# Block compression of a sparse attention: windows as the stationary operand, four positions at once in the column groups of TensorE

## What is computed

```python
def compress(k, pos_emb, w1, w2):
    B, S, G, d = k.shape                                   # 1, 256, 2, 128
    nc = (S - CMP_LEN) // CMP_STRIDE + 1                   # 15
    idx = jnp.arange(nc)[:, None] * CMP_STRIDE + jnp.arange(CMP_LEN)[None, :]
    blocks = k[:, idx] + pos_emb[:, None, :]
    blocks = jnp.transpose(blocks, (0, 3, 1, 2, 4)).reshape(B, G, nc, CMP_LEN * d)
    return jax.nn.gelu(blocks @ w1, approximate=True) @ w2
```

## Time and profile before

| | |
|---|---|
| time, 3 runs | 2612.89 us median (2609.93 to 2614.18) |
| profiled execution: span, first to last instruction | 2603.2 us |
| median of the runs less this span | 9.7 us |
| TensorE busy | 2440.9 us, 94% |
| TensorE's weight loads | 2054.4 us, 79% |
| VectorE / ScalarE / GpSimd busy | 1418.9 / 1154.4 / 81.2 us |
| mean granted clock of TensorE | 0.955 |
| DMA | 418.71 MB, 161 GB/s in the mean |

### The profile page before, as it was taken

The page is one execution under the profiler, slowest core; times in us unless marked ns, Lnnn a source line. Parts: engine busy times, 40 slices in busy tenths (PEclk is TensorE's granted clock), DMA queues, the critical chain, the costliest instruction groups (busy, mean ns, idle before and its releaser), DMA issues.

```text
span 2603.2 us, 34397 instructions
## 1 busy us (share of the span) xinstructions
PE 2440.9 (94%) x12224; PEld 2054.4 (79%) x12224; DVE 1418.9 (55%) x1718; ACT 1154.4 (44%) x1620; POOL 81.2 (3%) x77
## 2 busy tenths in 40 slices
PE   6999987889999999999979996869899999999997
PEld 5887886768888788888868885658788888888886
DVE  4444336556666545666554445885555544455544
ACT  4444224445555444554444444334444444444432
POOL 1000100000000000000000001320000000000000
PEclk9999758989999999999989998889899999999999
DMA  7665330545555565665656652004466566665663
GB/s 228 193 191 163 98 129 5 166 130 186 186 185 175 190 192 171 193 193 193 191 159 189 193 161 65 1 25 153 128 186 185 186 192 190 190 185 182 208 193 105
DMA packets 298549, 418.71 MB, mean 161 GB/s; under 512 B 15263, under 2 KB 181465, under 8 KB 297701
## 3 DMA queue, kind: packets, MB, share of 16 engines
q1 hardware_dynamic: 295744, 407.09, 50.5%
q0 software_dynamic: 2144, 8.40, 1.0%
q10 hardware_dynamic: 580, 2.20, 0.2%
HBM read 415.52 MB, written 2.12 MB: 160 GB/s over the span
## 4 chain that ended last, share of the span: by engine, by line
PE 84%; issue 8%; DVE 5%; ACT 2%; POOL 1%; DMA 0%; ACTq 0%; DVEq 0%; POOLq 0%
PE PS L1289 22%; PE PS L1257 14%; PE PS L1256 14%; PE PS L1255 14%; PE PS L1290 11%; PE PS L1367 2%; PE PS L1302 1%; PE PS L1528 1%; DVE x L930 1%; DVE attT L1195 1%; DVE proj L1188 0%; PE PS L1304 0%; DVE proj L1192 0%; PE PS L1407 0%; PE PS L1344 0%
## 5 line engine op out<-in xcount | busy, mean ns | idle before, releaser
L806 DVE TENSOR_TENSOR wlo<-stage,whi 128x1024 fp32r<-128x1024 f32 (+2 forms) x452 | 540.3, 1199 | 625.1 <-ACT whi L529 625.0
L1289 PE MATMUL PS<-actT,whi 128*128 128x512 f32 x2432 | 859.7, 397 | 0.0
L529 ACT ACTIVATE whi<-stage 128x1024 fp32r<-128x1024 f32 (+2 forms) x452 | 467.2, 1037 | 679.6 <-PE PS L1257 656.4
L1290 PE MATMUL PS<-actT,wlo 128*128 128x256 f32 x2432 | 683.4, 281 | 0.0
L1289 PEld LDWEIGHTS PS<-actT,whi 128*128 128x128 f32 x2432 | 457.2, 188 | 112.9
L835 DVE TENSOR_TENSOR wlo<-stage,whi 128x1024 fp32r<-128x1024 f32 x298 | 358.5, 1223 | 232.5 <-ACT whi L580 230.3
L1290 PEld LDWEIGHTS PS<-actT,wlo 128*128 128x128 f32 x2432 | 456.5, 188 | 0.1
L580 ACT ACTIVATE whi<-stage 128x1024 fp32r<-128x1024 f32 x298 | 309.0, 1055 | 271.1 <-PE PS L1290 256.7
L1257 PE MATMUL PS<-whi,actT 128*128 128x512 f32 (+2 forms) x992 | 384.5, 388 | 0.0
L1255 PE MATMUL PS<-whi,actT 128*128 128x512 f32 (+2 forms) x992 | 383.8, 387 | 0.0
L1256 PE MATMUL PS<-wlo,actT 128*128 128x512 f32 (+2 forms) x992 | 381.7, 385 | 0.0
(11 more groups left out here) (249 smaller groups left out, 1605.3 us busy)
## 6 DMA issues: line engine op xcount, KB each, us to landing
stage<-in_w_up SPq DMA_DIRECT2D x304, 512.0 KB, 4.3
stage<-in_w_down SPq DMA_DIRECT2D x216, 512.0 KB, 4.7
stage<-in_w_in SPq DMA_DIRECT2D x168, 512.0 KB, 3.5
stage<-in_w_out SPq DMA_DIRECT2D x64, 512.0 KB, 4.8
stage<-in_cmp_k_w SPq DMA_DIRECT2D x8, 512.0 KB, 4.1
stage<-in_cmp_v_w SPq DMA_DIRECT2D x8, 512.0 KB, 5.1
x<-in_x ACTq DMA_DIRECT2D x2, 1024.0 KB, 6.9
grow<-bias_by_distance POOLq DMA_DIRECT2D x2, 1024.0 KB, 7.7
```

The lines of the kernel that those rows point to most:

```text
L529: nc.scalar.activation(whi[:, s % SPLITS, 0:wd], stage[:, s % STAGES, 0:wd], ACT.Copy)\
L806: nc.vector.tensor_tensor(wlo[:, s % SPLITS, 0:wd], stage[:, s % STAGES, 0:wd], whi[:, s % SPLITS, 0:wd].bitcast(F32), ALU.subtract).then_ ...
L1289: nc.tensor.matmul(o, whi[:, j % SPLITS, at], actT[:, k, :], start=k == 0, stop=False)
L1290: last = nc.tensor.matmul(o[:, S:2 * S], wlo[:, j % SPLITS, at], actT[:, k, 0:S], start=False, stop=k == KC - 1)
```

## The change

The operands of the first product change places. The 32 window columns of one position (2 groups x 16, the sixteenth a column of zeros) are now the stationary operand, and the 256 weight columns of that position move. A product with 32 stationary columns fills a quarter of the array's columns; the four positions of a tile are written to four column groups, that is to PSUM partitions 0-31, 32-63, 64-95 and 96-127 of one bank (bank 6 for keys, 7 for values). Each group sums its own eight positions, so four partial sums remain, with windows on partitions and hidden units along the row.

ScalarE copies these partial sums to SBUF (`part`), for the keys in step 4 and the values in step 8. In step 8 four small products with four stacked 32 x 32 identities (`stack`) add the four partial sums and turn the result at once (`hidden`); one gelu then covers keys and values. The window row in SBUF is now 32 wide, with a memset for the zero column, and `stack` is a further DMA at the start.

```diff
+    c["stack"] = np.tile(np.eye(32, dtype=np.float32), (4, 1))
...
+        part = sb("part", [P, 2, HID], F32, mixer1)
+        stack = sb("stack", [P, 32], F32, mixer1)
...
+            pool.dma_start(stack[:, :], w["stack"]).then_inc(ev("stack_in"), 16)
             for j, nm in enumerate(("lambda_q1", "lambda_q2", "lambda_k1", "lambda_k2")):
...
             pool.wait_ge(ev("cols"), 1)
+            pool.memset(blocks[:, :, :, :, NC:NC + 1].rearrange("p v l g c -> p (v l g) c"), 0.0).then_inc(ev("blocks_done"), 1)
...
-                        pool.tensor_tensor(blocks[:, v, 16 * a:16 * a + 16, g, :], src, add, ALU.add).then_inc(ev("blocks_done"), 1)
+                        pool.tensor_tensor(blocks[:, v, 16 * a:16 * a + 16, g, 0:NC], src, add, ALU.add).then_inc(ev("blocks_done"), 1)
...
                     act.wait_ge(ev("tile_used"), used(G["cmp"].first + STAGES * (v + 1)))
-                    nc.scalar.activation(hid[:, v, :, :], PS[:, 6:8, 0:2 * NC], ACT.Gelu_apprx_tanh).then_inc(ev("hid_done"), 1)
+                    nc.scalar.activation(part[:, v, :], PS[:, 6 + v, 0:HID], ACT.Copy).then_inc(ev("part_out"), 1)
                 if s == 8:
+                    act.wait_ge(ev("hidden_mm"), 1)
+                    nc.scalar.activation(hid, PS[:, 6, 0:P].rearrange("p (v a c) -> p v a c", v=2, a=2),
+                                         ACT.Gelu_apprx_tanh).then_inc(ev("hid_done"), 1)
...
+            def hidden():
+                pe.wait_ge(ev("part_out"), 2)
+                for n in range(4):
+                    last = nc.tensor.matmul(PS[:, 6, n * 32:(n + 1) * 32], part[:, n // 2, n % 2 * P:(n % 2 + 1) * P], stack[:, :],
+                                            start=True, stop=True)
+                last.then_inc(ev("hidden_mm"), 1)
...
-                    pe.wait_ge(ev("blocks_done"), 4 * (v + 1))
-                    if v:
-                        pe.wait_ge(ev("hid_done"), 1)
+                    pe.wait_ge(ev("blocks_done"), 4 * (v + 1) + 1)
...
                             k = FC * (j % STAGES) + l
-                            for a in range(2):
-                                at = stage[:, j % STAGES, l * HID + a * P:l * HID + (a + 1) * P]
-                                last = nc.tensor.matmul(PS[:, 6 + a, 0:2 * NC], at,
-                                                        blocks[:, v, k, :, :].rearrange("p g c -> p (g c)"),
-                                                        start=k == 0, stop=k == CMP_LEN - 1)
+                            last = nc.tensor.matmul(PS[32 * l:32 * l + 32, 6 + v, 0:HID],
+                                                    blocks[:, v, k, :, :].rearrange("p g c -> p (g c)"),
+                                                    stage[:, j % STAGES, l * HID:(l + 1) * HID],
+                                                    start=j % STAGES == 0, stop=j % STAGES == STAGES - 1)
...
                 if s == 8:
+                    pe.wait_ge(ev("stack_in"), 16)
+                    hidden()
                     pe.wait_ge(ev("w2_in"), 32)
-                    pe.wait_ge(ev("hid_done"), 2)
+                    pe.wait_ge(ev("hid_done"), 1)
```

More of the change, by code:

```diff
@@ L189, in build @@
         urow = work[0:16, 2048:2048 + SK]
-        blocks = grow[:, 0:2 * CMP_LEN * NKV * NC].rearrange("p (v l g c) -> p v l g c", v=2, l=CMP_LEN, g=NKV)
+        blocks = grow[:, :].rearrange("p (v l g c) -> p v l g c", v=2, l=CMP_LEN, g=NKV)
         w2 = proj[:, 0, C_KC:C_KC + 512].rearrange("p (v a n) -> p v a n", v=2, a=2)
-        hid = proj[:, 1, C_KC:C_KC + 4 * 2 * NC].rearrange("p (v a c) -> p v a c", v=2, a=2)
-        kcT = proj[:, 1, C_KC + 128:C_KC + 128 + 2 * NC]
+        hid = proj[:, 1, C_KC:C_KC + 4 * 32].rearrange("p (v a c) -> p v a c", v=2, a=2)
+        kcT = proj[:, 1, C_KC + 128:C_KC + 128 + 32]
         vc = proj[0:NC, 1, C_KC + 192:C_KC + 192 + NKV * P].rearrange("p (g d) -> p g d", g=NKV)
@@ L1008, in compressed @@
                     dve.wait_ge(ev("kc_mm"), 1)
-                    nc.vector.tensor_copy(kcT, PS[:, 7, 0:2 * NC])
+                    nc.vector.tensor_copy(kcT, PS[:, 7, 0:32])
                     nc.vector.tensor_copy(vc, PS[0:NC, 7, 2 * P:4 * P].rearrange("p (g d) -> p g d", g=NKV)).then_inc(ev("kc_out"), 1)
@@ L1364, in compress @@
                             k = FC * (j % STAGES) + l
-                            for a in range(2):
-                                at = stage[:, j % STAGES, l * HID + a * P:l * HID + (a + 1) * P]
-                                last = nc.tensor.matmul(PS[:, 6 + a, 0:2 * NC], at,
-                                                        blocks[:, v, k, :, :].rearrange("p g c -> p (g c)"),
-                                                        start=k == 0, stop=k == CMP_LEN - 1)
+                            last = nc.tensor.matmul(PS[32 * l:32 * l + 32, 6 + v, 0:HID],
+                                                    blocks[:, v, k, :, :].rearrange("p g c -> p (g c)"),
+                                                    stage[:, j % STAGES, l * HID:(l + 1) * HID],
+                                                    start=j % STAGES == 0, stop=j % STAGES == STAGES - 1)
                         last.then_inc(ev("tile_used"), 1)
                 if s == 8:
+                    pe.wait_ge(ev("stack_in"), 16)
+                    hidden()
                     pe.wait_ge(ev("w2_in"), 32)
-                    pe.wait_ge(ev("hid_done"), 2)
+                    pe.wait_ge(ev("hid_done"), 1)
                     for a in range(2):
-                        nc.tensor.matmul(PS[:, 7, 0:2 * NC], w2[:, 0, a, :], hid[:, 0, a, :], start=a == 0, stop=a == 1)
+                        nc.tensor.matmul(PS[:, 7, 0:32], w2[:, 0, a, :], hid[:, 0, a, :], start=a == 0, stop=a == 1)
                     for g in range(NKV):
                         for a in range(2):
-                            last = nc.tensor.matmul(PS[0:NC, 7, (2 + g) * P:(3 + g) * P], hid[:, 1, a, g * NC:(g + 1) * NC],
+                            last = nc.tensor.matmul(PS[0:NC, 7, (2 + g) * P:(3 + g) * P], hid[:, 1, a, g * 16:g * 16 + NC],
                                                     w2[:, 1, a, :], start=a == 0, stop=a == 1)
@@ L1386, in compress @@
                         last = nc.tensor.matmul(PS[:, 7, n * 16:n * 16 + NC], QT[:, 16 + h, t * P:(t + 1) * P],
-                                                kcT[:, g * NC:(g + 1) * NC], start=True, stop=True)
+                                                kcT[:, g * 16:g * 16 + NC], start=True, stop=True)
                     last.then_inc(ev("cmp_mm"), 1)
```

## The result

| | before | changed |
|---|---|---|
| time, median (4 runs each) | 2612.84 us (2609.93 to 2614.18) | 2569.02 us (2568.06 to 2570.31) |
| ratio | | 0.9838, 95% interval 0.9818 to 0.9857 |
| profiled execution: span | 2603.2 us | 2567.5 us |
| profiled execution: its own time | not given | 2569.29 us |
| mean granted clock | 0.955 | 0.963 |

The change is 43.8 us faster by the medians, 37 to 48 us by the interval of the ratio; the forecast was 38 us (2575). Between the two profiled executions the span shrank by only 35.7 us. Experiment 1 is about this gap of 8 us.

What follows compares the result with a forecast made beforehand. TensorE's compression, mostly at 1.2 GHz, was taken to bound steps 0 to 7 of the first attention. -39.2 + 0.8 + 0.4 = -38 us; 2603.2 - 38 + 9.7 = 2575 us, inner range 2572 to 2578, wide range 2567 to 2588.

Steps and rivals of the forecast that it cites:

- rival 4: More gained: steps 8 to 10 also at the high clock, or a better clock for the next GEMM; 2569 to 2572 us, 12%.
- The compression on TensorE: First product in steps 0 to 7: four column groups run at once, 0.9 us a step plus 0.15 at each of two switches.
- C: Compression part of one step on TensorE at the high clock: 0.86 us if four run at once, 3.44 if none overlap.
- Rival 1: Column groups run in turn at the high clock: TensorE's step is 5.6 us and binds; 2586 us, 15%.
- The binding loop: Steps 0 to 7: addition, exponentials, ScalarE's copy, transposes, next addition bind next, 4.28 + 0.05 + 0.58 = 4.9 us a step.
- the stretch: First attention, score addition of step 0 to that of step 7: 70 us before, 39.2 us less after.
- Step 8: After the eighth score addition: copy, four products, table load and gelu cost 0.45 to 1.2 us more; 0.8 taken.
- What costs nothing: GpSimd's memset, the stacked identity's DMA and second-half weights: done or landed in time; DMA bytes could cost some tenths.
- Clock: High level expected in steps 0 to 7; steps 8 to 10 up to 4 us less or 2 more, 0.4 us added.
- Rival 2: Packed, but the clock stays at 1.2 GHz through steps 1 to 7, TensorE's step 5.5 us; 2581 us, 12%.
- The sum: Whole kernel: -39.2 + 0.8 + 0.4 = -38 us; span 2603.2 - 38 = 2565.2, plus 9.7 around the span, 2575 us.

Runs made afterwards that it cites:

- Experiment 1: The kernel before, unchanged, run once more as a yardstick: 2611.33 us, ratio 1.0003; its profiled execution had a span of 2606.2 us.
- experiment 2: The changed kernel with all 64 compression products in one column group instead of four: 2578.72 us, ratio 0.9886 to the kernel before.
- experiment 4: The changed kernel with only the first of four positions of each tile multiplied, in one column group: 2569.36 us, ratio 0.9840 to the kernel before.
- experiment 3: The changed kernel with two column groups instead of four, each summing two positions of a tile: 2571.26 us, ratio 0.9857 to the kernel before.
- experiment 7: The changed kernel with ScalarE's copy of transposed probabilities ahead of the exponentials: 2562.02 us, ratio 0.9813 to the kernel before.
- experiment 5: The kernel before with compression records moving 128 columns instead of 30, same stationary operands: 2583.72 us, ratio 0.9897 to the kernel before.
- experiment 6: The changed kernel, unchanged, run again as a yardstick: 2569.12 us beside 2612.30 for the kernel before, ratio 0.9836.

## Why the prediction was right, and where it was off

The time lies in the stated range (2567 to 2588), but 6 us below the forecast, outside its inner range of 2572 to 2578, and where rival 4 had put it (2569 to 2572). The mechanism of rival 4 did not come: from the addition of step 7 to the end the changed kernel's profiled execution takes 1.25 us more than that of before, not less. By the prediction's own steps:

- **The compression on TensorE.** C was taken at 0.9 us with 0.3 for switches. Measured: 1.07 us for sixteen records, and 0.33 us of idle ahead of them. Four column groups do run at once (experiments 2 and 4). The Trainium skill (TensorE: Matmul & The Clock Gate, Part 3) says that weight loads overlap with running matmuls only when the row group differs; here the trace disagrees, since all loads share all rows and 16 of them fit into the 1.07 us of the products (0.59 us of PEld in the row of 312.20). The Trainium skill's figure there is 2.38 for three column tiles, 0.79 a tile. Here 3.57 us for one group against 1.07 is 3.3 for four, 0.83 a tile, with a modelled end in the 1.07; by the starts, four every 0.22 us, it is close to four. So the trace has no less a tile than that figure, and the 1.4 us that the prediction made of it by keeping 2.38 for four was too long. Rival 1 was wrong as a forecast but right as a price (experiment 2).
- **The binding loop.** Right in kind (experiments 3, 4 and 7) and 0.3 us too short: 5.2 us a step instead of 4.9. The terms that were mis-sized are the 0.05 us between copy and transposes (measured 0.14) and the 0.58 us from there to the addition (0.63 at the high level, 0.84 to 0.98 at the low one). Both are visible in the chain above: 0.14, 0.82 and 0.09 us between 333.35 and 334.40. The 4.28 us up to the end of the copy came out as priced (329.07 to 333.35), so a step at the high level takes 5.05 us, and the three with low-level transposes 5.26 to 5.39. With 0.2 us more in the first two steps, that is 37.4 us less in the stretch instead of 39.2.
- **Step 8.** 0.33 us more, where 0.45 to 1.2 was priced: the table load (349.40 to 350.68) did lie beside the four products (349.53 to 350.58), and neither waited for the other.
- **What costs nothing.** GpSimd's memset took 0.34 us and no one waited for it. While the weights of the second half came, the DMAs moved 258 GB/s at first; they were in time, 6.9 us from issue to landing instead of 5.1.
- **Clock.** Right in direction. The level was not high throughout: it fell in three pieces of the stretch, 0.82 in the mean from 323 to 345 us. Behind it, where 4 us less or 2 more were thought possible, it was 0.61 to 374.5 us, against 0.68 before. Rival 2, the low level throughout, did not come; experiment 5 shows why the reading behind it (the level was low here before) did not carry over: that level belonged to the records with 30 moving columns.
- **The sum.** Within the profiled execution the working was off by 2.3 us: 2603.2 - 38 = 2565.2, against a measured span of 2567.5. Of this, 1.8 us are the stretch and 0.5 lie ahead of it (its first addition is at 312.31 instead of 311.82). Behind it 1.25 us were added, where the prediction had 0.8 + 0.4. The step that failed is the one that carried this to the median of the runs: "9.7 us more, which lies around the span". What lies around the span is 1.8 us; the profiled execution of before was one of about 2605.0 us, 7.8 us under the median. The misreading alone costs nothing, since the median less 38 is 2575 too. What it hid is that the saving came from one quick execution and was taken as the same in all. The two profiled executions of before spent 70.0 and 73.6 us in the stretch, those of the changed kernel 32.5 and 32.2: it saved 37.4 us in the first pair and 41.3 in the second (experiments 1 and 6, both some 3.5 us under their medians, with spans 42.4 us apart). So a larger saving in the stretch is probably the greater part of the miss. That it is the whole is not shown: outside the stretch, too, executions differ by several us either way. The two errors, 2.3 and about 8 us, have opposite signs, so that the forecast is only 6 us off is in part luck.

What stays open: where the rest of before's spread comes from, since only two of its executions were profiled, 3.6 us apart in the stretch; and whether the changed kernel spreads less. Before ranged over 4.3 us in the four runs of the result and over 9 to 12 us where 9 to 17 runs were taken, and the changed kernel, never run more than five times together, over 2 to 6.

## What to carry to other kernels

Where a stage runs at the low clock and its matmul records take as long with few moving columns as with many, try swapping the operands or widening the moving one first: here the clock that it brought was worth more (28.6 us) than the packing (10 to 13). When the dominant engine of a stage is relieved, write out the loop of the others link by link, with its semaphores; here an order of two instructions on ScalarE showed no gain in steps 0 to 7 before the change and 3.3 us after it. And compare the span of a profiled execution with its own time before a sum is built on it. If that execution is not a typical one, profile another: a saving measured in one of them need not be that of the median.

## What the runs showed of the hardware

- Four products in the four column groups, each with all 128 rows and its own moving operand, start together, within 20 ns: 16 records of 256 columns in 1.07 us, against 3.57 us in one group.
- A kernel with 256 records of 128 stationary fp32 columns was 28.6 us faster when each moved 128 columns instead of 30. At 2.4 GHz such a record takes 0.118 and 0.115 us.
- With two column groups the clock was 1.00 over steps 0 to 7; with four it dipped, to 0.88 and 0.89 over the stretch, though the loop is the same. With a quarter of the products it dipped likewise (0.84). One execution of each was profiled here (two with four groups), so this is an observation and not a rule.
